# DeltaNet mixer of a transformer block: unscaled keys and queries, both tiles in three blocks

## The reference, cut to what matters

```
qkv, z, ga, gb = split(u @ w_in)                  # 8 heads of 128, 256 tokens
qkv  = silu(causal_depthwise_conv(qkv, conv_w))
q, k = l2norm(q), l2norm(k)                       # t * rsqrt(sum(t*t) + 1e-6)
beta = sigmoid(gb);  g = -exp(a_log) * softplus(ga + dt_bias)
decay[i,j] = exp(cumsum(g)[i] - cumsum(g)[j]) for i >= j, else 0
A = I + strict_lower((k*beta) @ k.T * decay)      # inverted per chunk
v_new = inv(A) @ (v*beta - (k*beta*exp(gc)) @ state)
o = (q*exp(gc)) @ state + (q @ k.T * decay) @ v_new
state = state*exp(g_last) + (k*exp(g_last-gc)).T @ v_new
o = rmsnorm(o, norm_w) * silu(z)                  # eps 1e-6, mean over 128
```

## Time and profile before

| | |
|---|---|
| median of 3 runs | 2760.13 us |
| the profiled execution | 2763.47 us |
| its span | 2761.8 us |
| PE busy | 2337.4 us (85%) |
| DVE busy | 1330.7 us (48%) |
| ACT busy | 807.1 us (29%) |
| mean granted TensorE clock | 0.893 |

### The profile page before, as it was taken

The page is one execution under the profiler, slowest core; times in us unless marked ns, Lnnn a source line. Parts: engine busy times, 40 slices in busy tenths (PEclk is TensorE's granted clock), DMA queues, the critical chain, the costliest instruction groups (busy, mean ns, idle before and its releaser), DMA issues. The chain is left out here.

```text
span 2761.8 us, 40825 instructions
## 1 busy us (share of the span) xinstructions
PE 2337.4 (85%) x17264; PEld 1888.0 (68%) x17264; DVE 1330.7 (48%) x1528; ACT 807.1 (29%) x966; POOL 21.5 (1%) x62
## 2 busy tenths in 40 slices
PE   5996659978898798699999999996978577888885
PEld 5996559958776665699999999985854433443442
DVE  3763445565525301588888879784552211111112
ACT  4443223332113301443434334434441111111110
POOL 0000000000000000000000000000000000000000
PEclk9997879978758899899999999998999568999997
DMA  4442003410004430588888888863432399999998
GB/s 177 182 182 119 2 1 122 182 54 3 2 1 163 173 122 0 232 334 332 314 327 329 317 329 331 339 229 145 183 122 89 135 370 412 428 427 427 428 428 344
DMA packets 68156, 610.12 MB, mean 221 GB/s; under 512 B 9614, under 2 KB 9870, under 8 KB 16782
## 3 DMA queue, kind: packets, MB, share of 16 engines
q1 hardware_dynamic: 56906, 572.11, 51.8%
q0 software_dynamic: 1872, 23.07, 2.1%
q10 hardware_dynamic: 9216, 12.60, 1.3%
HBM read 674.85 MB, written 14.68 MB: 250 GB/s over the span
## 5 line engine op out<-in xcount | busy, mean ns | idle before, releaser
L1759 ACT ACTIVATE ffn_w_hi<-ffn_raw 128x2048 fp32r<-128x2048 f32 x128 | 245.0, 1916 | 371.2 <-PE psum L1804 367.9
L1766 DVE TENSOR_TENSOR ffn_w_lo<-ffn_raw,ffn_w_hi 128x2048 fp32r<-128x2048 f32 x128 | 292.3, 2287 | 88.9 <-ACT ffn_w_hi L1759 88.9
L1802 PE MATMUL psum<-u_hi,ffn_w_hi 128*128 128x256 f32 x1024 | 293.5, 287 | 15.1 <-DVE ffn_w_lo L1766 14.0
L2511 PE MATMUL psum<-moe_raw,moe_x_t 128*32 128x512 f32 x1536 | 219.3, 703 | 87.6 <-DMA moe_raw<-in_moe 80.0
L1804 PE MATMUL psum<-u_hi,ffn_w_lo 128*128 128x256 f32 x1024 | 293.0, 286 | 0.0
L1803 PE MATMUL psum<-u_lo,ffn_w_hi 128*128 128x256 f32 x1024 | 292.9, 286 | 0.0
L591 DVE SCALAR_TENSOR_TENSOR shared<-mod_raw,c_silu,shared 128x2048 f32<-128x2048 f32 x96 | 225.1, 2344 | 0.0
L1802 PEld LDWEIGHTS psum<-u_hi,ffn_w_hi 128*128 128x128 f32 x1024 | 199.8, 195 | 15.9 <-DVE ffn_w_lo L1766 14.2
L1803 PEld LDWEIGHTS psum<-u_lo,ffn_w_hi 128*128 128x128 f32 x1024 | 199.6, 195 | 0.4
L1804 PEld LDWEIGHTS psum<-u_hi,ffn_w_lo 128*128 128x128 f32 x1024 | 199.6, 195 | 0.0
L1802 PE MATMUL psum<-ffn_w_hi,ffn_hid_hi 128*128 128x512 f32 x512 | 199.5, 390 | 0.0
(11 more groups left out here) (537 smaller groups left out, 4491.2 us busy)
## 6 DMA issues: line engine op xcount, KB each, us to landing
moe_raw<-in_moe SPq DMA_DIRECT2D x96, 2048.0 KB, 17.4
ffn_raw<-in_ffn SPq DMA_DIRECT2D x128, 1024.0 KB, 5.0
ring<-in_stream SPq DMA_DIRECT2D x59, 2048.0 KB, 12.3
mod_raw<-in_mod SPq DMA_DIRECT2D x96, 1024.0 KB, 7.3
moe_raw<-in_moe POOLq DMA_DIRECT2D x48, 2048.0 KB
expert_rows<-moe_stage ACTq DMA_DIRECT2D x192, 64.0 KB, 8.4
x<-in_x SPq DMA_DIRECT2D x2, 1024.0 KB, 8.0
mem<-in_mem SPq DMA_DIRECT2D x2, 1024.0 KB, 15.0
```

The source lines that it names most:

```text
L1759: act.activation(self.w_hi[:, number % self.HIGHS], self.raw[:, number % self.RAWS], ACT.Copy)\
L1766: dve.tensor_tensor(self.w_lo[:, number % self.LOWS], self.raw[:, number % self.RAWS], self.w_hi[:, number % self.HIGHS].bitcast(F32), ALU ...
L1802: pe.matmul(out, lhs[0], rhs[0], start=start, stop=False)
L2511: mm = pe.matmul(summed(tile)[strip(q), :], e.x_t[:, tile // 4 % 2, UNIT_KC * u + c, strip(tile % 4)], w[:, c * COLS:(c + 1) * COLS], star ...
```

## The change: what it does, and the diff

1. `w_gate` is loaded by `begin`, between the second and third unit of the stream; its own block is gone. The gate products (`gates`) run on PE inside the block of `split_input`.
2. q and k stay as they come from the projection, features on partitions. Their squares are taken by ACT (`act_after` 24 and 25), summed over the partitions by 32 matmuls with a column of ones (`pe_after` 27), and the roots of all 32 sums (2 x 2 x 8) are taken once. The norms and beta are applied as per-row factors: `w` = beta / |k|^2 in the product matrix and in v_new, |k| into v (`v_rows`), the q norm only in the output's norm (`q_sq`, `q_inv`).
3. All of that, the gates' functions, the transposes of k (tile 0) and v (both tiles) and the first `decays` stand between the products of the last eight projection tiles: `pe_after`, `act_after`, `dve_after`.
4. After the projection there are three blocks for both tiles together: `deltanet_products`, `invert` (one call, two groups of 8 heads, one group per tile) and `deltanet_chain`.

The three engines' hooks in the projection:

```diff
+    def gates(self, pe):
+        pe.wait_ge(k.small_in, 16)
+        for t in range(TT):
+            for c in range(KC):
+                mm = pe.matmul(bank(k, 6 + t)[:, 0:16], self.u[:, c, t * P:(t + 1) * P], self.w_gate[:, c, :],
...
+    def pe_after(self, pe, m):
+        if m == 27:
+            pe.wait_ge(k.act_sem, self.z_act["k_squared"])
...
+            mm.then_inc(k.pe_sem, 1)
+            pe.wait_ge(k.dve_sem, self.z_dve["g1"])
+            turn(8, 0, 4)
+            turn(12, 0, 6)
+        if m == 28:
+            turn(16, 0, 7)
+        if m == 29:
+            pe.wait_ge(k.turn_taken, k.turns + 1)
+            turn(20, 0, 4)
+            pe.wait_ge(k.turn_taken, k.turns + 2)
+            turn(16, 1, 6)
+        if m == 30:
+            pe.wait_ge(k.act_sem, self.z_act["root"])
+            turn(20, 1, 5)
+    def act_after(self, act, m):
+        if m in (24, 25):
+            act.activation(self.squares[:, 8 * n:8 * n + 8], qkvz[:, 8 * n:8 * n + 8], ACT.Square)
+        if m == 26:
+            act.activation(self.beta[:], self.beta[:], ACT.Sigmoid)
+        if m == 27:
+            act.activation(self.g[:], self.g[:], ACT.Exp)
+            act.activation(self.a_exp[:], ..., ACT.Exp)
+        if m == 28:
+            act.activation(self.g[:], self.g[:], ACT.Ln, bias=k.one[:, 0:1])
+        if m == 29:
+            act.wait_ge(k.pe_sem, self.z_pe["ssq"])
+            act.activation(self.root[:]..., bank(k, 5)[:, 0:32], ACT.Sqrt, bias=k.eps[:, 0:1])
+    def dve_after(self, dve, m):
+        if m == 25:
...
+        if m == 28:
...
+        if m == 29:
+            dve.wait_ge(k.act_sem, self.z_act["ln"])
...
+        if m == 30:
+            dve.wait_ge(k.act_sem, self.z_act["root"])
...
+        if m == 31:
...
```

```diff
+                deltanet_products(nc, k, net, Xs, [bufs[t][2][:] for t in range(TT)], bufs[1][3][:])
+                invert(nc, k, Xs, groups)
+                deltanet_chain(nc, k, net, Xs, [bufs[t][0] for t in range(TT)], [a for b in bufs for a in b[1:]], mixed)
```

In `deltanet_products` PE does the decays of tile 0, the running sums, the 8 products of tile 0, the decays of tile 1 and its 8 products; ACT does five Exp and then scales k of tile 0 (8 times 128x128); DVE makes both matrices, per tile one mask (128x1024), 8 steps of 128x128 and 4 of 128x256. In `deltanet_chain` every step is split in two halves of 4 heads with a semaphore each:

```diff
+            for g in range(2):
+                product(g, g, lambda h: Us[0][:, h, :], dn.v_tm[0])
+            for g in range(2):
+                pe.wait_ge(k.dve_sem, on_dve[f"v0{g}"])
+                product(4 + g, g, lambda h: dn.k_tm[:, h, :], v0)
+            for g in range(2):
+                product(2 + g, g, lambda h: Xs[0][:, h, 1, :], v0)
+            for g in range(2):
+                pe.wait_ge(k.act_sem, on_act[f"s{g}"])
+                product(6 + g, g, lambda h: qkvz[:, 8 + h, tokens(1)], state)
+            for g in range(2):
+                product(g, g, lambda h: qkvz[:, h, tokens(1)], state)
+            for g in range(2):
+                pe.wait_ge(k.dve_sem, on_dve[f"r{g}"])
+                product(4 + g, g, lambda h: Us[1][:, h, :], dn.v_tm[1])
+            for g in range(2):
+                pe.wait_ge(k.dve_sem, on_dve[f"v1{g}"])
+                product(6 + g, g, lambda h: Xs[1][:, h, 1, :], v1)
```

More of the change, by code:

```diff
@@ new lines, in products @@
+            def products(t):
+                for n, b in enumerate(banks[t]):
+                    if t and n:
+                        pe.wait_ge(k.dve_sem, on_dve[f"q0{n - 1}"])
+                    for h in (2 * n, 2 * n + 1):
+                        own = slice(t * P, t * P + P)
+                        mm = pe.matmul(bank(k, b)[:, h % 2 * T:h % 2 * T + T], qkvz[:, 8 + h, own], at[:, :, h, own],
+                                       start=True, stop=True)
+                    mm.then_inc(k.pe_sem, 1)
@@ L721, in _, with decay @@
[L721 to L727, removed]
+            def decay(t):
+                for b in range(2):
+                    act.wait_ge(k.pe_sem, on_pe[f"dec{t}{b}"])
+                    act.activation(flat(dec[t][:, 4 * b:4 * b + 4, :]), bank(k, 4 + b), ACT.Exp).then_inc(k.act_sem, 1)
@@ L747, in _ @@
         @block.scalar
         def _(act):
[L749 to L753, removed]
+            for g in range(2):
+                act.wait_ge(k.pe_sem, on_pe[f"s{g}"])
+                act.activation(state[:, mine(g)], heads(4 + g), ACT.Copy).then_inc(k.act_sem, 1)
@@ L755, in _ @@
+            act.wait_ge(k.dve_sem, on_dve["mean1"])
+            act.activation(dn.o_ssq[:, 1], dn.o_ssq[:, 1], ACT.Sqrt, bias=k.eps[:, 0:1]).then_inc(k.act_sem, 1)
         @block.vector
@@ L781, in deltanet_prepare @@
[L781 to L799, removed]
@@ new lines, in scaled @@
+                for g in range(2):
+                    s.step(dve.tensor_tensor(own[t][:, mine(g)], own1[:, mine(g)] if t else heads(2 + g),
+                                             over(dn.o_ssq[:, t, mine(g)]), ALU.mult))
+            for g in range(2):
+                weighted(0, g, g)
+            for g in range(2):
+                dve.wait_ge(k.pe_sem, on_pe[f"ks{g}"])
+                for h in range(4):
+                    row = dn.v_tm[1][:, 4 * g + h, :]
+                    rest = dve.scalar_tensor_tensor(row, bank(k, 6 + g)[:, h * P:(h + 1) * P], dn.less[:, 4 * g + h:4 * g + h + 1],
+                                                    row, ALU.mult, ALU.add)
+                s.step(rest)
@@ new lines, in _ @@
+            for g in range(2):
+                dve.wait_ge(k.pe_sem, on_pe[f"qs{g}"])
+                s.step(dve.tensor_tensor(own1[:, mine(g)], heads(g), over(dn.sums[:, 1, mine(g)]), ALU.mult))
+            for g in range(2):
+                weighted(1, g, 4 + g)
+                summed(0, g)
+            mean(0)
+            for g in range(2):
+                dve.wait_ge(k.pe_sem, on_pe[f"o1{g}"])
+                s.step(dve.tensor_tensor(own1[:, mine(g)], own1[:, mine(g)], heads(6 + g), ALU.add))
```

446 lines of the change are left out of this document (235 added, 211 removed).

## The result

The kernel with the change takes 2689.35 us (median of 4 runs, 2687.06 to 2691.78), beside 2760.18 us for the kernel before on the same chip (4 runs, 2759.71 to 2763.82): ratio 0.9737, interval 0.9724 to 0.975, so 70.8 us less. The forecast was 2693.

What follows compares the result with a forecast made beforehand. PE bounds the projection; no engine fills the stages from 229 to 403 us. There 172.9 us become 25 + 14.6 + 40.3 + 27.5, less 1.3 at the start: 66.8 won, forecast 2693 us, range 2680 to 2709.

Steps and rivals of the forecast that it cites:

- start, gained: Before the projection: split begins 5.1 us earlier, gate products lengthen its block by 3.8; 1.3 us gained.
- tail, added: Last projection tiles: narrow matmuls, transposes, table loads, waits and half clock add 25 us, bounds 17 to 38.
- products of both tiles: Joint products block after the projection: 14.6 us with the barrier, against 23.8 before; bounds 12.5 and 20.
- inversion: One joint inversion on two groups of 8 heads: 40.3 us against 45.1 before; bounds 39 and 42.
- chain: Joint chain of both tiles, last changed block: 27.5 us against 58.4 before; bounds 23 and 36.
- RWKV split earlier by: End of the changed stages, 403 us before: everything after them starts 66.8 us earlier.
- One-column matmuls: Behind product 27: 32 matmuls summing the squares take 9.0 us, bounds 7 and 14.
- three waits for `low`: In the projection's tail: PE waits 0.6, 3.3 and 3.0 us for `low`, in product 29 and ahead of 30 and 31.
- the clock loss of product 30: In the tail, after the wait ahead of product 30: 3 us at half clock cost 1.5 us.
- upper bound of 38: Tail's worst case, 38 us: sums take 14 us and the clock stays low from product 28 to the end.
- Rival B: Tail costs more: each switch holds ACT another load, 2701 us, or clock low through products 28 to 31, 2706; chance 0.13.
- Rival C: Joint blocks keep PE fast, narrow products fast: products 13, chain 23.5, tail 20, total 2683 us; chance 0.12.

Runs made afterwards that it cites:

- first profile: The changed kernel's first profiled execution, nothing further altered: projection's first `high` at 42.12 us, RWKV split at 333.6 us, span 2685.4 us.
- second profile: The changed kernel run and profiled again, nothing altered: first `high` at 38.96 us, RWKV split at 330.93 us, median 2687.21 us.
- experiment 1: Changed kernel with its 32 one-column matmuls in four runs of eight behind products 25 to 28: 2689.95 us, tail 59.9 us in place of 61.4.
- experiment 3: Changed kernel with gate products turned, 16 gate columns stationary and 256 tokens moving: 2684.20 us, first `high` 5.4 us earlier than in its first profile.
- experiment 9: Changed kernel with each one-column matmul moving 128 columns into a scrap bank: tail 58.4 us in place of 61.4; total 2654.32 us, not comparable.
- experiment 2: Changed kernel with DVE's hooks of tiles 29 and 30 behind the next tile's `low`, last four transposes behind product 31: 2676.85 us, tail 52.5.
- experiment 4: Changed kernel with Sigmoid, Exp, Ln and Sqrt in the hooks replaced by Square, removing eight table loads: tail 55.0 us in place of 61.4; total not compared.
- Experiment 5: Changed kernel with the inversion called once per tile, two groups of four heads each: 2692.61 us, inversion 45.5 us against 40.35.
- experiment 12: Changed kernel with spread sums, turned gates, DVE hooks behind the next `low` and late Silus, run a second time: 2670.54 us, ratio 0.9665.
- the kernel with all four rearrangements: Changed kernel with spread sums, turned gates, DVE hooks behind the next `low` and late Silus: 2670.43 us, ratio 0.9672; again, 2670.54 us.

## Why the prediction was right

By its steps, in the time of each profile:

| step | forecast | measured |
|---|---|---|
| start, gained | 1.3 | -1.7 (first profile), 1.4 (second) |
| tail, added | 25 | 25.0 |
| products of both tiles | 14.6 | 14.0 |
| inversion | 40.3 | 40.35 |
| chain | 27.5 | **22.45** |
| RWKV split earlier by | 66.8 | 69.25 (first profile), 71.95 (second) |

- **Start.** The bounds held, and so did both halves of the reasoning: the split 4.6 us earlier, the gate products longer than the split. (10.2 less 6.9 is 3.3, not the 3.8 of the prediction; its 3.8 holds with 0.5 us of barrier that it doesn't name, and 0.5 was measured, 41.64 to 42.12.) Their length depends on when the clock falls: 12.65 us in one profile, 10.78 in the other, forecast 10.2. Over eight profiles with these gate products and an unchanged start the first `high` lies at two places, near 39.0 or between 41.95 and 42.3. The sign of this step cannot be told from one profile.
- **Tail.** The mechanism was right, queue by queue. That the sum was right to 0.1 is luck: its terms were off by up to 1.5 us, in both directions. One-column matmuls 9.9 (9.0), transposes behind them 1.95 (1.8), product 28 at half clock until 221.3, 1.2 (1.5), three waits for `low` 5.8 (0.6 + 3.3 + 3.0), root 1.6 (1.1), product 31 at half clock for 4.5 us, 2.2 (1.5). Not there: the clock loss of product 30 (1.5); from its first matmul on, 236.69 to 240, the clock is 1.00. In experiments 1, 3 and 9 that loss is there. Experiments 2 and 4 bear out that the waits come from the order and the loads. The upper bound of 38 does not follow from the terms given for it: 5 us for the sums and 192 matmuls at 0.12 in place of 4.5, another 18.5, make some 48, less what waits they would cover. Rival B had both the switch at two loads' price and the clock low through four products: neither is seen.
- **Products and inversion.** As worked out. Experiment 5 shows that the joint call is worth 5.1 us by itself, against 4.8 forecast. How much of that is fewer stretches at the low clock (two inversions had one each, of 3 and 7 us, the joint one had one of 7) is not separated.
- **Chain: the term that failed,** below its lower bound of 23. The prediction put "w0 at half clock, 3.6", "w1 is done at 14" and the end at 25.5, and then took 27.5, with no row for the addition. In the trace each product follows the one before without a wait: w0 1.9 us (forecast 3.6), s 1.9 (2.9), o0, ks and qs 5.4 (5.7), w1 1.95 (1.9), done 11.1 us from the start, at 322.3 (14 forecast), with v0 on DVE beside w0 and s. From there to the end are 11.3 us, against 11.5 forecast. So of the 5 us 2 are the unfounded addition and 3 lie ahead of w1's end. Experiments 5 and 12, where the clock did fall, put w1's end at 12.6, so 1.5 of the 3 are the clock; the other 1.5 are w0, s and the three products behind them, each priced a little too high even for a chain that starts slow. Why the clock stays up in ten profiles with groups of eight and falls in the eleventh is open. The prediction's "every barrier of before is followed by clock 0.50" is a misreading: the product behind the barrier at 316.98, in the 1.00 window of the earlier trace rows, took 2.0 us for its 16 instructions. Rival C had the clock right for products and chain, and was wrong for the tail.
- **Total.** 69.25 at the split and 70.8 in the medians agree within the scatter of the last stage. At the split the forecast was 2.5 us short: 5 from the chain and 0.6 from the products, less 3 from the start in that profile. So part of the nearness is luck: with the start of the second profile it is 5.2 short. The other 1.2 of the 3.7 between 2693 and 2689.35 are scatter of the runs.

## What to carry to other kernels

Work hung between the tiles of a PE-bound loop is priced by the queues it stands in: put each step that waits for a slow result behind the next tile's own step, and do that before making anything faster (9.3 us here, by order alone, where faster sums alone gave 1.5 to 3.0). Do not take a clock from another stage as given: write both sums, with it high and low. Compare profiles at the last milestone that the change can reach: the DMA-bound stage behind it scattered by 7 us. Then compare the changed stage itself, for the stretches ahead of it scattered by up to 3 us.

## What the runs showed of the hardware

- PE busy without a gap does not keep the granted clock. Behind 64 instructions with one moving column it stands at 0.50, behind as many with 128 it stays at 1.00, and the longer instructions end sooner: 7.3 us against 9.9. The gate products, 16 moving columns, took 10.4 to 13.1 us over eight profiles, and 7.1 with 256 columns and half the matmuls.
- Matmuls whose outputs overlap in one bank kept their rate: 32 in 7.31 us where each is shifted by a column, 7.30 where all write the same columns. That is 0.114 us per instruction, as the 48 transposes of the earlier trace rows to columns of their own (0.113).
- Where the clock falls differs between profiles of one and the same kernel, and nothing in its code decides it. The first `high` came at 39.0 or 42.1 us in the changed kernel; the kernel with all four rearrangements had a fall in the tail and none in the chain in one profile, and the reverse in the other.
